# Feed-forward pre-norm of a hybrid encoder layer: normalised rows made from the turned residual and a turned scale, in place of being turned themselves

## The reference, cut to what matters

```python
    mix = jnp.concatenate([pool_out, attn_out], axis=-1) @ w_out
    x = x + rms_norm(mix, ln_mix_post)          # x1
    h = rms_norm(x, ln_ffn_pre)                 # h2 = x1 * (1 / rms of the token) * gain of the channel
    f = (jax.nn.silu(h @ w_gate) * (h @ w_up)) @ w_down
    x = x + rms_norm(f, ln_ffn_post)
```

## Time and profile before

| | |
|---|---|
| median of 3 runs | 2474.73 us (2473.93 to 2476.96) |
| profiled execution, its own time | 2474.1 us |
| span of its rows | 2472.3 us |
| TensorE busy | 2377.4 us (96%) |
| VectorE / ScalarE / GpSimd busy | 68% / 43% / 36% |
| granted TensorE clock, mean | 0.987 |
| output projection stage | about 691 to 903 us of the span |
| hand-over to the steady feed-forward | about 903 to 947 us |

### The profile page before, as it was taken

The page is one execution under the profiler, slowest core; times in us unless marked ns, Lnnn a source line. Parts: engine busy times, 40 slices in busy tenths (PEclk is TensorE's granted clock), DMA queues, the critical chain, the costliest instruction groups (busy, mean ns, idle before and its releaser), DMA issues.

```text
span 2472.3 us, 30578 instructions
## 1 busy us (share of the span) xinstructions
PE 2377.4 (96%) x11520; PEld 1976.2 (80%) x11520; DVE 1676.5 (68%) x1783; ACT 1071.1 (43%) x1585; POOL 885.9 (36%) x541
## 2 busy tenths in 40 slices
PE   7999899999979998999999999799999999999998
PEld 6888688888868876888888888688788888878787
DVE  6666688888844547777676556687888865574832
ACT  4333588888844444333333222444433332234322
POOL 0000144534402333454344265354456634640300
PEclk9999999999989998999999999999999999999999
DMA  4111211100047675454456865755457587666431
GB/s 148 35 43 60 72 37 44 39 31 24 20 145 223 190 220 180 132 170 149 150 166 262 316 230 182 227 179 187 163 174 263 200 333 267 243 223 224 151 96 54
DMA packets 327633, 386.48 MB, mean 156 GB/s; under 512 B 17216, under 2 KB 239296, under 8 KB 327360
## 3 DMA queue, kind: packets, MB, share of 16 engines
q1 hardware_dynamic: 327488, 384.53, 46.4%
HBM read 247.12 MB, written 137.36 MB: 156 GB/s over the span
## 4 chain that ended last, share of the span: by engine, by line
PE 84%; DVE 5%; DMA 3%; issue 2%; SPq 2%; ACT 2%; POOL 1%; POOLq 0%; DVEq 0%; ACTq 0%
PE ps L1284 44%; PE ps L1060 31%; PE ps L1063 9%; DMA stg<-h_forms 2%; DVE ring L1991 1%; SPq L597 1%; DVE reg L2000 1%; SPq L579 1%; DMA xb<-x_turned 0%; DMA f_turned<-ev 0%; DVE win L1871 0%; DMA stg<-mix_turned 0%; DVE fb L2289 0%; DVE x2l L2132 0%; DVE fhi L2111 0%
## 5 line engine op out<-in xcount | busy, mean ns | idle before, releaser
L1284 PE MATMUL ps<-reg,ring 128*128 128x512 f32 x5544 | 1274.4, 392 | 34.7 <-DVE ring L1991 32.9
L1284 PEld LDWEIGHTS ps<-reg,ring 128*128 128x128 f32 x5544 | 1048.2, 189 | 260.1 <-DVE ring L1991 30.8
L1401 ACT ACTIVATE ring<-wraw 128x1024 fp32r<-128x1024 f32 (+2 forms) x152 | 143.5, 946 | 380.1 <-PE ps L1284 377.9
L1991 DVE TENSOR_TENSOR ring<-wraw,ring 128x1024 fp32r<-128x1024 f32 (+2 forms) x152 | 227.6, 1498 | 60.8 <-ACT ring L1401 60.0
L1060 PE MATMUL ps<-win,ht 128*128 128x512 f32 (+1 forms) x1152 | 231.9, 360 | 4.8 <-DVE win L1871 4.8
L1060 PEld LDWEIGHTS ps<-win,ht 128*128 128x128 f32 x1152 | 189.7, 191 | 34.9 <-issue 4.4
L1401 ACT ACTIVATE ring<-ws 128x1024 fp32r<-128x1024 f32 (+2 forms) x114 | 107.9, 947 | 240.2 <-PE ps L1284 232.9
L1942 DVE TENSOR_TENSOR pt<-ps,pt 128x512 fp32r<-128x512 f32 x256 | 173.0, 687 | 47.4 <-ACT pt L1401 43.0
L1991 DVE TENSOR_TENSOR ring<-ws,ring 128x1024 fp32r<-128x1024 f32 (+2 forms) x114 | 176.3, 1547 | 40.3 <-ACT ring L1401 39.5
L1060 PE MATMUL ps<-wout,ct 128*128 128x512 f32 x768 | 183.3, 395 | 10.6 <-DVE wout L1958 10.6
L1401 ACT ACTIVATE pt<-ps 128x512 fp32r<-128x512 f32 x256 | 153.7, 601 | 64.3 <-PE ps L1063 60.7
(11 more groups left out here) (211 smaller groups left out, 3032.0 us busy)
## 6 DMA issues: line engine op xcount, KB each, us to landing
reg<-ff_forms SPq DMA_DIRECT2D x42, 1536.0 KB, 10.6
ff_forms<-fhi SPq DMA_DIRECT2D x88, 512.0 KB, 3.2
wraw<-in_w_gate SPq DMA_DIRECT2D x88, 256.0 KB, 4.2
wraw<-in_w_up SPq DMA_DIRECT2D x88, 256.0 KB, 4.7
ff_forms<-ev SPq DMA_DIRECT2D x44, 512.0 KB, 2.9
wraw<-in_w_down SPq DMA_DIRECT2D x48, 384.0 KB, 5.5
stg<-h_forms SPq DMA_DIRECT2D x28, 512.0 KB, 5.8
reg<-ff_forms SPq DMA_DIRECT2D x14, 1024.0 KB, 6.3
```

Source lines behind the costliest of these rows:

```text
L1284: last = nc.tensor.matmul(ps[:, 2 * chain + m, :], ring[:, st % 3, a, m, k * P:(k + 1) * P], reg[:, k, i, e, :], start=OPENS[i] and k == 0 ...
L1401: copy = lambda out, src, **k: nc.scalar.activation(out, src, ACT.Copy, **k)
L1991: V.tensor_tensor(ring_block(u, st, 1), weight_source(u, i), f(ring_block(u, st, 0)), ALU.subtract).then_inc(S["w_split"], 1)
```

## The change

The h2 rows are no longer made and turned. GpSimd multiplies the turned residual `x1t` by the gain, now one column for each channel block (`xg`). VectorE spreads the token's scale over 128 columns (`rows_r`), TensorE turns that once into its own PSUM bank, and VectorE multiplies `xg` by it into `h2a` or `h2b`. `xg` and `rows_r` have one buffer each.

```diff
-        gffn = sb(s_d, "gffn", [P, D])
+        gffn = sb(s_d, "gffn", [P, KT])
+        rows_r = sb(s_d, "rows_r", [P, P])
-        h2 = sb(s_d, "h2", [P, D])
+        xg = sb(s_d, "xg", [P, KT, P])
...
# SP
-            sp.dma_start(gffn[:], g_ffn_pre.partition_broadcast(P)).then_inc(S["gains_in"], 16)
+            with nc.allow_non_contiguous_dma(reason="gain columns, loaded once"):
+                sp.dma_start(gffn[:], g_ffn_pre.rearrange("(k p) -> p k", p=P)).then_inc(S["gains_in"], 16)
...
# GpSimd
-            for pair in range(NT):
+            def forms_made(pair):
                 b = pair % 2
                 lo, hi, made = h2a[:, b], h2b[:, b], forms[:, b]
...
+            for n in range(NSEQ * NT):
+                pool.wait_ge(S["x1_out"], n + 1)
+                pool.wait_ge(S["h2_out"], n)
+                nc.gpsimd.tensor_tensor(xg[:], x1t[:], gffn[:].unsqueeze(2).to_broadcast([P, KT, P]), ALU.mult)\
+                    .then_inc(S["h2_ready"], 1)
+                if n >= 3 and n % 2:
+                    forms_made(n // 2 - 1)
+                if n == 9:
                     pool.wait_ge(S["strip_split"], 2 * KT)
                     alone(pool)
                     for which in range(3):
                         sums(UNITS[0], which)
-                if pair == NT - 2:
-                    pool.wait_ge(S["w_split"], 2)
-                    sums(UNITS[0], 3)
+            forms_made(NT - 1)
+            pool.wait_ge(S["w_split"], 2)
+            sums(UNITS[0], 3)
...
# TensorE
+            def turn_back(n):
+                pe.wait_ge(S["x1_ready"], n + 1)
+                pe.wait_ge(S["x1_out"], n)
                 for k in range(KT):
-                    last = turn(ps[:, 5 + k // 4, (k % 4) * P:(k % 4 + 1) * P], src[:, k * P:(k + 1) * P])
-                last.then_inc(S[("x1_turned", "h2_turned")[which]], 1)
+                    last = turn(ps[:, 5 + k // 4, (k % 4) * P:(k % 4 + 1) * P], x1[:, k * P:(k + 1) * P])
+                last.then_inc(S["x1_turned"], 1)
+                pe.wait_ge(S["x1_scale"], n + 1)
+                pe.wait_ge(S["h2_out"], n)
+                turn(ps[:, 7, 0:P], rows_r[:]).then_inc(S["h2_turned"], 1)
...
             for n in range(1, NSEQ * NT):
                 mix_half(n, 0)
-                if n >= 2:
-                    turn_back(n - 2, 1)
                 mix_half(n, 1)
-                turn_back(n - 1, 0)
-            turn_back(NSEQ * NT - 2, 1)
+                turn_back(n - 1)
...
-            turn_back(NSEQ * NT - 1, 0)
+            turn_back(NSEQ * NT - 1)
             product(UNITS[0], 0)
-            turn_back(NSEQ * NT - 1, 1)
...
# ScalarE: h2_out is gone from its list (16 copies), and
             def x1_out(n):
                 act.wait_ge(S["x1_turned"], n + 1)
                 act.wait_ge(S["x1_stored"], n * 16)
+                act.wait_ge(S["h2_ready"], n)
...
# VectorE, post_a: the wait on h2_ready is gone; post_b and the new h2_out:
-                V.scalar_tensor_tensor(out=h2[:], in0=x1[:], scalar=small[:, 7:8], in1=gffn[:],
-                                       op0=ALU.mult, op1=ALU.mult).then_inc(S["h2_ready"], 1)
+                V.tensor_copy(rows_r[:], small[:, 7:8].to_broadcast([P, P])).then_inc(S["x1_scale"], 1)
+
+            def h2_out(n):
+                dve.wait_ge(S["h2_ready"], n + 1)
+                dve.wait_ge(S["h2_turned"], n + 1)
+                b = n // 2 % 2
+                dve.wait_ge(S[f"h2_st{b}"], 16 * NP * (n // 4))
+                at = (h2a, h2b)[n % 2][:, b]
+                V.tensor_tensor(at, xg[:], ps[:, 7:8, 0:P].to_broadcast([P, KT, P]), ALU.mult).then_inc(S["h2_out"], 1)
...
                 if n:
                     post_b(n - 1)
+                if n >= 2:
+                    h2_out(n - 2)
...
             post_a(NSEQ * NT - 1)
             fill_lo(0, 0)
             post_b(NSEQ * NT - 1)
+            h2_out(NSEQ * NT - 2)
             fill_lo(0, 1)
+            h2_out(NSEQ * NT - 1)
```

More of the change, by code:

```diff
@@ L299, in encoder_layer @@
         ct_1 = sb(s_d, "ct_1", [P, 2, KT, P], F32R)
-        gffn = sb(s_d, "gffn", [P, D])
+        gffn = sb(s_d, "gffn", [P, KT])
+        rows_r = sb(s_d, "rows_r", [P, P])
+        sb(s_d, "gffn_rest", [P, D - KT - P])
         junk_d = sb(s_d, "junk_d", [P, D], BF16)
         sb(s_d, "stg_d", [P, 3 * 2 * CH])
-        h2 = sb(s_d, "h2", [P, D])
+        xg = sb(s_d, "xg", [P, KT, P])
         s_d.close()
@@ L370, in encoder_layer @@
             "gains_in", "c_hi", "c_split", "mix_done", "m_sum", "m_root", "mix_read", "x1_ready",
-            "x1_sum", "x1_root", "h2_ready", "x1_turned", "x1_out", "h2_turned", "h2_out", "x1_stored",
+            "x1_sum", "x1_scale", "x1_root", "h2_ready", "x1_turned", "x1_out", "h2_turned", "h2_out", "x1_stored",
             "h2_forms", "h2_st0", "h2_st1", "eps_set", "ones_set", "raw_w0", "raw_w1", "w_sums", "w_hi",
@@ L1022, in _ @@
                     .then_inc(S["h2_forms"], 1)
-                if pair == 3:
+            pool.wait_ge(S["gains_in"], 32)
+            alone(pool)
+            for n in range(NSEQ * NT):
[6 more added lines that the diff above has]
+                if n == 9:
                     pool.wait_ge(S["strip_split"], 2 * KT)
@@ L1242, in mix_half @@
                     mix_strip(n, c, k)
[L1244 to L1252, removed]
-                for k in range(KT):
-                    last = turn(ps[:, 5 + k // 4, (k % 4) * P:(k % 4 + 1) * P], src[:, k * P:(k + 1) * P])
-                last.then_inc(S[("x1_turned", "h2_turned")[which]], 1)
+            def turn_back(n):
+                pe.wait_ge(S["x1_ready"], n + 1)
+                pe.wait_ge(S["x1_out"], n)
+                for k in range(KT):
+                    last = turn(ps[:, 5 + k // 4, (k % 4) * P:(k % 4 + 1) * P], x1[:, k * P:(k + 1) * P])
[3 more added lines that the diff above has]
+                turn(ps[:, 7, 0:P], rows_r[:]).then_inc(S["h2_turned"], 1)
             pe.wait_ge(S["c_split"], 1)
@@ L1296, in _ @@
             pe.wait_ge(S["ones_set"], 1)
-            turn_back(NSEQ * NT - 1, 0)
+            turn_back(NSEQ * NT - 1)
             product(UNITS[0], 0)
-            turn_back(NSEQ * NT - 1, 1)
             pe.wait_ge(S["mix_read"], NSEQ * NT)
             product(UNITS[0], 1)
+            pe.wait_ge(S["x1_out"], NSEQ * NT)
             pe.wait_ge(S["h2_out"], NSEQ * NT)
@@ L1687, in _ @@
                     concat_hi(n + 1)
-                if n >= 2:
-                    h2_out(n - 2)
                 if n:
@@ L1697, in _ @@
             fill_hi(0, 0)
-            h2_out(NSEQ * NT - 2)
             post_b(NSEQ * NT - 1)
@@ L1701, in _ @@
             fill_hi(0, 1)
-            h2_out(NSEQ * NT - 1)
             for st in range(-2, NST + 1):
@@ L1968, in post_a @@
                 dve.wait_ge(S[f"xd_in{n % 2}"], (n // 2 + 1) * 16)
-                dve.wait_ge(S["h2_ready"], n)
                 dve.wait_ge(S["x1_turned"], n)
```

## The result

The changed kernel takes 2483.61 us (median of 8 runs, 2482.01 to 2489.9) against 2475.32 us for the kernel before (8 runs, 2473.93 to 2479.55). The ratio is 1.0034, with a 95% interval of 1.0023 to 1.0044: slower by 8.3 us. The profiled execution took 2483.81 us, 9.7 more than that of before, with a span of 2482.0.

What follows compares the result with a forecast made beforehand. TensorE, busy for 96% of the span, bounds the kernel; a closed loop of 27.2 us a pair would exceed its 23.8. Tile 15 7.6 us late plus 14.4 in the hand-over gave 22.0 on 2474.1: 2497 us, range 2481 to 2508.

Steps and rivals of the forecast that it cites:

- the price of the form stores: SP's stores of a pair's forms: 6.6 us in the loop, 7.7 us for pair 6 in the hand-over.
- TensorE's saving: TensorE loses 14 runs of 8 transposes and gains 15 single ones in the loop: net 10.5 us less.
- Forms in front of SP, the closed loop: Late GpSimd forms delay SP's stores and the input load behind them, then scale and next `xg`: 27.2 us a pair.
- The loop as the pair's length: Tiles 7 to 15: four pairs at the loop's 27.2 us against 25.34 before, 7.4 us, plus 1.2 for weight subtractions.
- The hand-over: Tile 15's start to the first product nothing holds up, before the feed-forward: 69.9 us in place of 55.5, 14.4 more.
- Rival C (the clock): Waits let TensorE's clock fall, every other pair takes 29.4 us, some 5 us more in all, 2502 us; chance 11%.
- Holds between GpSimd and VectorE: The engines exclude each other where VectorE reads two SBUF tiles: 0 to 2.5 us on the forms, 2.05 taken.
- The hold on the scale's copy: One GpSimd instruction could hold up VectorE's spread of the scale, up to 1.3 us a tile; not in the sum.

Runs made afterwards that it cites:

- e7: Changed kernel with SP's form stores directly behind the input load of tile 2*pair+7, pair 6 as before; 2474.51 us, ratio 0.9994 to the kernel before.
- e2: Changed kernel with GpSimd making a pair's forms ahead of `xg(n)` in place of behind it, in the whole stage; 2470.73 us, ratio 0.9988 to the kernel before.
- e11: Changed kernel with 36 dummy transposes on TensorE ahead of the scale wait behind tiles 6 and 10; 2483.88 us, ratio 1.0034 to the kernel before.
- e1: Changed kernel with SP's form stores one tile later, behind the next input load; 2478.48 us, ratio 1.0016 to the kernel before.
- e4: Kernel before the change with SP's form stores one tile later; 2490.9 us, ratio 1.0071 to the kernel before.
- e6: Changed kernel with forms ahead of `xg` only for n = 13 and 15 (pairs 5 and 6, the hand-over); 2475.63 us, ratio 1.0002 to the kernel before.

## Why the prediction was wrong

The direction, the mechanism and its places were as forecast, and 2483.6 lies inside the range of 2481 to 2508; but 22.0 us were forecast and 8.3 measured (9.7 between the two profiled executions). The steps that failed are the price of the form stores, 6.6 and 7.7 us where they took 5.1, and the step from the loop's length to the pair's. By the steps of the sum:

- **TensorE's saving.** 0.87 us for each run of transposes and 0.11 for the single one: from tile 1's product to tile 4's it took 2.3 us less, as worked out. Held.
- **Forms in front of SP, the closed loop.** Held, link by link, in the order given. e7 shows it from SP's side, e2 from GpSimd's. What failed are sizes. The loop was set at 27.2 us; it took 24.7 (789.15 to the end of `h2_out` at 813.74, and 0.1 to hand over). Forms 9.1 in place of 10.05: `xg` took 1.90, not the 2.41 of a sum of two full tiles, and the rest 7.2, not 7.65. The seven form stores took 5.1 us in place of 6.6. Landing 6.3 (6.1), ScalarE's copy to the end of `h2_out` 4.0 (4.3).
- **The loop as the pair's length.** This was a further step too simple. At 24.7 the loop is close to what TensorE needs, and TensorE needs more than 23.8 where its clock fell in the wait (25.8 from tile 7 to 9). So the two alternate as the bound: 25.8, 26.2, 25.4, 27.8 us, the last with the weight subtractions, in which the loop itself took 26.2 (867.96 to 894.18). Where TensorE is late, `xg` is late too (2.6 us at 816.37, 2.3 at 867.96), and the next loop starts from there. 8.6 were forecast, 3.8 measured. That this is no farther off is in part luck: with the loop at 24.7 the prediction's own sum, 4 x (24.7 - 25.34) + 1.2, gives a gain of 1.4 us. Pricing the loop too high hid 5.2 us that the sum had no term for.
- **The hand-over.** All links as forecast, 14.4 us against 8.0. From tile 15's start: forms of pair 5 ready at 8.2 (9.3), stores 5.1 (6.6), landing 6.1 (6.2), copy to `h2_out` 4.2 (4.3), `xg` and forms 10.2 (10.5), stores 5.1 (7.7), the remaining chain 24.9 (25.3). **The largest mis-sized term is the form stores: 4.1 of the 6.2 us here, and 1.5 a pair in the loop.** Their 6.6 and 7.7 were read where SP issued them right behind other transfers; now SP comes to them after a pause of 8 to 10 us, and the first two take 0.9 to 1.1 us in place of 1.9 to 2.1. That the pause is the reason is argued from the rows of all the traces (below); no run changed it alone.
- **Rival C (the clock)** had the mechanism right as well: e11 shows that the wait causes the slow product, and the pair behind it is TensorE's, with no wait at its end. Its price was too high: it put 5.6 us on TensorE's part of such a pair, where the slow products of tiles 7 and 11 took 2.0 and 1.6 more. But part of it comes through, 1.8 us up to tile 11 by e11's rows. What it adds to the whole isn't settled.
- **Holds between GpSimd and VectorE** were put at 0 to 2.5 a pair, 2.05 in the sum. The forms took 7.2 us with them against 5.45 without: 1.75.

The hold on the scale's copy, which the prediction told of only by the Trainium skill, can be seen in the changed kernel's timeline, where GpSimd is idle and where it is at work:

```profile
787.64 0.23 DVE L1977 COPY rows_r<-small 128x128 f32<-128x128 f32 x1
...
794.70 2.04 POOL L1024 TENSOR_TENSOR forms<-h2b,forms 128x512 f32<-128x512 f32 x1 [0.18 <-POOL forms L1023]
795.71 1.12 DVE L1977 COPY rows_r<-small 128x128 f32<-128x128 f32 x1
796.75 1.21 DVE L1986 TENSOR_TENSOR h2b<-xg,ps 128x1024 f32<-128x1024 f32 x1
796.92 1.30 POOL L1025 TENSOR_TENSOR forms<-h2a,forms 128x512 f32<-128x512 f32 x1 [0.18 <-POOL forms L1024]
```

0.23 us alone and 1.12 beside L1024; `h2_out`, with one operand in PSUM, takes 1.21 either way. The page that the prediction named (Trainium skill, GPSIMD Engine Reference, Key points) tells of contention between GpSimd and VectorE instructions in a 2-port mode or with two SBUF inputs. The trace agrees for `h2_out`, which is not held; in which mode the copy runs no row tells. In the changed kernel the hold cost nothing: every held copy is that of a tile with room (TensorE came for this scale at 803.16), and the copies ahead of TensorE's waits took 0.23. In e2 it did cost: ahead of the wait at tile 12 the copy took 2.21 us beside a weight sum.

## What to carry to other kernels

When a step is moved to another engine, look up what that engine's list already holds and who consumes its results in order: here 1.9 us of new work, put ahead of an old step, made the old step wait for what the new one waits for and moved a whole queue of transfers by 9 us, and one swap of two entries turned a loss of 8 us into a gain of 3. Before a queue's entry is moved, look for the buffer that it frees as well as for the one that it fills (e1, e4). A chain of links has to be priced with durations from the conditions that it will meet, and compared with the next bound close under it: 27.2 us forecast for the loop put it clear above TensorE's 23.8, and at the 24.7 measured the two take turns.

## What the runs showed of the hardware

- The same seven stores took SP 6.6 us right behind the store of `x1t` in the loop of the kernel before (1.9 us for the first two) and 5.0 to 5.1 after a pause of 6 to 12 us (0.9 to 1.1 for the first two), in every trace here with such a pause. Single issues in the chain of the changed kernel rise from 0.38 to 0.89 us.
- After waits of 4.2 to 5.2 us at tile 7, 48 matmuls took 12.4 to 13.2 us in place of 11.2. After waits of about 2 us they were slow in some places (12.76 behind 2.15, in the changed kernel) and not in others (11.16 behind 2.02, in e6). The granted clock from 789.4 to 797 was 0.73 in the changed kernel and 1.00 in e11.
- A GpSimd product of a full tile with a gain repeated along the row took 1.90 us, a sum or difference of two full tiles 2.4.
